# Token factor and shift applied to the result of two units at each norm boundary, and one unit per head pair moved from attention to the delta rule

## The chip, the cores and the metric

The kernel runs on one core of one Trainium2 chip. The metric is the device time of one execution in microseconds (us). Engines are named as in the profile: PE (TensorE; PEld its weight loads), DVE (VectorE), ACT (ScalarE), POOL (GpSimd), SP (SyncE, which issues the loads).

## The reference, cut to what matters

One decoder layer over 512 tokens of width 1024, all in float32:

```python
mod = cond @ w_ada[l] + b_ada[l]          # nine vectors: shift, scale, gate for each of three norms
u = modulate(rms_norm(h, g_ffn1[l]), sh1, sc1)            # rms_norm * (1 + scale) + shift
h = h + 0.5 * gt1 * swiglu(u, w_ffn1_in[l], w_ffn1_out[l])
u = modulate(rms_norm(h, g_mix[l]), sh2, sc2)
h = h + gt2 * hybrid_mixer(u, ...)        # stick-breaking attention | gated delta rule, merged by sigmoid gates
u = modulate(rms_norm(h, g_ffn2[l]), sh3, sc3)
h = h + 0.5 * gt3 * swiglu(u, w_ffn2_in[l], w_ffn2_out[l])
```

The mixer projects u to q, k, v of attention (8 heads of 64), to q, k, v, z, b, a of the delta rule (4 heads of 128) and to 2 x 1024 gate columns. For one token t, the modulated input is u = r(t) * (h * g * (1 + scale)) + shift, with one number r(t) per token. So a projection of it is u @ W = r(t) * ((h * g * (1 + scale)) @ W) + shift @ W.

## The kernel before, in words

Activations lie transposed: hT, u_hi and u_lo are [128 features, 8 chunks, 512 tokens]. Each matrix product is made of units. A unit is 128 output columns: its weights come by DMA into one of four `raw` slots, ACT rounds them to fp32r (`split_hi`, w_hi, L562), DVE forms the rest (`split_lo`, w_lo, L953), both into one of two slots, and PE runs three matmuls for each of 8 chunks (L1416 to L1418: w_hi u_hi, w_hi u_lo, w_lo u_hi; 11 chunks for a half unit of the FFN's second product). A unit's split waits until the unit two before it has freed the slot. Units have one numbering through the program: F1_IN, F1_OUT (first FFN), SB_IN (12 units: q, k, v of attention), DN_IN (the list MIXED: the delta rule's projections and the 16 gate units), MERGE, W_OUT, F2_IN, F2_OUT. Every engine has its own written-out program and meets the others at semaphores; SP issues the loads in the order of the units, each after the DVE split that frees its slot (`load_next`), and each gate unit's store before the load that follows it.

**Norm boundaries.** At F1_OUT to SB_IN and at W_OUT to F2_IN the next input needs the norm of the whole of h. After each output chunk DVE adds it to hT (`residual`, L1040) and ACT squares it (L569); POOL sums seven of eight squares. `statistics` makes two matmuls with 512 columns each (fp32, two passes each: L1427, L1429), which put the mean on all 128 partitions; `rough_root` (ACT, Ln and Exp, L574, L576) and `newton` (DVE, three operations, L990 to L994) work on [128, 512]. Then `norm` makes one chunk after another: `scaled` (DVE, L1027), u_hi (ACT, adds the shift, L593), `low` (DVE, u_lo, L1021), and `two_units` (L1445 to L1447) runs the first two units chunk by chunk as they come. While this goes on PE has nothing else.

**The conditioning vectors.** The 7168 late columns of w_ada are scaled by ACT (L582), halved by DVE (L961) and summed by PE (`ada_total`, L1434, one matmul for every four pieces); in F1_OUT that matmul stands between the two half units of every second output chunk.

**Attention.** For each of four head pairs: `scores` (L1614, L1618), then ACT's Abs, Exp, Ln and DVE's max-add (L1208), ACT's copy to att_hi (L766) and DVE's att_lo (L1214), then the log weights on PE (L1628), Exp (L770), the values (L1663), and ACT's and DVE's copy of y (L773, L1227). While PE waits for those it runs chunks of the MIXED units (`shadow`): 20 before the log weights, 6 before the values, 6 after them, four units for each pair. SHADOW holds these numbers; all three engines follow them through `pair_unit`.

**Delta rule.** Its stretch is serial work in small tiles: silu of the convolved q, k, v (ACT, L785, L786), l2 norms of q and k in four steps (squares L794, PE L1692, roots L807 and L811, DVE `newton` and L1244), transposes of v and k (L1700, L1708), then for each two blocks of 128 tokens the decay matrices, a triangular inverse in levels and the state steps. Between its steps PE runs the rest of MIXED: z units in the first three l2 steps, then gate units in numbers of chunks that the table FILL gives for each point; the class `filler` lets ACT and DVE make their part of a unit (split of the unit after next, eviction) when its eighth chunk is reached.

Of the kernel before, what the change touches and what calls it, by code (L numbers as in the profile page):

```python
# [54 lines left out]
    + [m for h in range(4) for m in (("conv", 5 + h), ("gate", h))] + [("z", h) for h in range(4)] \  # L55
    + [("gate", g) for g in range(4, 16)]
# [3 lines left out]
FILL_0 = Z_0 + 4  # L60
# [4 lines left out]
SHADOW = {"keep": 20, "weights": 6, "y": 6}  # L65
FILL = {"l2": 8, "start": 8, "prep": 7, "inv0": 2, "norm": 4, "level": 2, "join": 1, "solve": 2, "solved": 2, "step": 1, "last": 2}
# [22 lines left out]
def pair_unit(p, n):  # L89

    return PAIR_0 + 4 * p + n
# [34 lines left out]
def build(nc, x, c, w_ada, b_ada, g_ffn1, w_ffn1_in, w_ffn1_out, g_mix, w_in, g_q_sb, g_k_sb, w_conv,  # L126
# [13 lines left out]
    with ExitStack() as ctx:  # L140
# [28 lines left out]
        share = sb("share", [P, 1])  # L169
        ssq = sb("ssq", [P, S])  # L170
# [4 lines left out]
        with ExitStack() as s:  # L175
# [7 lines left out]
            tok = {n: sb("tok_" + n, [P, NB], stack=s) for n in ("sum", "mean", "rstd", "tmp")}  # L183
        with ExitStack() as s:
            g_hi, g_lo = sb("g_hi", [P, KF, S], f32r, stack=s), sb("g_lo", [P, KF, S], f32r, stack=s)
            with ExitStack() as t:
                ada_raw = sb("ada_raw", [P, 2, KD, P], stack=t)
            with ExitStack() as t:
                out_nat = sb("out_nat", [P, 2, NB, P], stack=t)
# [50 lines left out]

        def heads(ap):
# [45 lines left out]
        stat_ps, root_ready, rstd_ready, refined = sem("stat_ps"), sem("root_ready"), sem("rstd_ready"), sem("refined")  # L287
# [44 lines left out]
        def gate_buffer(g):  # L332

            return gate_out if g >= DNH and g % 2 else rstd
# [19 lines left out]
        def _(sp):  # L354
# [84 lines left out]
            for i in laps(sp, KD // 2, 0, 1):  # L439
                for u in range(4):  # L440
                    load_next(F1_OUT, i, u)
                    if not (is_static(i) and i == KD // 2 - 1 and u >= 2):
                        load_late(2 * KF + 4 * i + u - 2, u % 2)
            for n in range(SB_IN, F2_IN):
# [11 lines left out]
                if MERGE + 2 <= n < MERGE + KD:  # L456
                    sp.wait_ge(part_ready, 2 * (n - MERGE - 1))
                    stored(sp, n + 1 - MERGE + KD)
                    load_gates(n - MERGE)
            for phase, steps in ((F2_IN, KF // 2), (F2_OUT, KD // 2)):  # L460
# [6 lines left out]
        def _(pool):  # L467
# [38 lines left out]
            pool.wait_ge(u_lo_ready, 2 * KD)  # L506
# [41 lines left out]
        def _(act):  # L548
# [36 lines left out]
            def rough_root(s):  # L585
                act.wait_ge(stat_ps, s)
                inverse_root(rstd[:, :], 4, root_ready, s - 1)

            def norm_hi(s):
                rough_root(s)  # L590
                for k in range(KD):
                    act.wait_ge(normed_ready, KD * s + k + 1)
                    act.activation(u_hi[:, k, :], work[:, k % 2, :], ACT.Identity,  # L593
                                   bias=mod[:, SH[s] * KD + k:SH[s] * KD + k + 1]).then_inc(u_hi_ready, 1)

            def ffn(f, phase):

                for i in laps(act, KF // 2):
                    for jj in range(2):
# [72 lines left out]
            for i in laps(act, KD // 2):  # L672
                for oo in range(2):
                    split_hi(F1_OUT, i, 2 * oo + 2)
                    split_hi(F1_OUT, i, 2 * oo + 3)
                    squares(1, 2 * i + oo, oo)
                    if not (is_static(i) and i == KD // 2 - 1 and oo):
                        for k in range(2):
                            ada_scale(ada_raw[:, k], ada_scaled, (ada_in[k], 16 * (KF + 2 * i + oo)))
# [14 lines left out]

            for n in range(12):
                split_hi(SB_IN, 0, n + 2)
                act.wait_ge(unit_done, SB_IN + n + 1)
                act.activation(sb_T[:, n, :] if n < 8 else v_T[:, n - 8, :], bank(6 + n % 2), ACT.Copy).then_inc(proj_ready, 1)
# [13 lines left out]
            def mixed(m):  # L712
# [16 lines left out]
                else:  # L729
                    stored(act, d if d < DNH + 2 else d - 1)  # L730
# [19 lines left out]
            for p in range(SBH // 2):  # L750
# [20 lines left out]
                mixed(pair_unit(p, 2))  # L771
                act.wait_ge(y_ps, p + 1)
                act.activation(ysb_hi[:, p, :], region[0][:, 0:S], ACT.Copy).then_inc(y_hi_ready, 1)  # L773
                mixed(pair_unit(p, 3))
# [11 lines left out]
            act.activation(conv[:, 8:12, :], conv[:, 8:12, :], ACT.Silu).then_inc(dn_silu, 1)  # L786
            act.preload_act_table_set("natural_log_exp_and_others")
# [1117 lines left out]
```

## Time and profile before

| | us |
|---|---|
| median of 3 timed runs (lowest, highest) | 1314.07 (1313.59, 1314.76) |
| the profiled execution, its own time | 1316.56 |
| its span in the profile | 1314.8 |
| PE busy | 1261.0 (96%) |
| PE weight loads busy | 1012.2 (77%) |
| DVE busy | 646.7 (49%) |
| ACT busy | 604.9 (46%) |
| POOL busy | 61.9 (5%) |
| chain that ended last, PE's share | 87% |

The span is from the first to the last instruction of the profiled execution. Busy shares are of the span. The granted TensorE clock (PEclk) is a share of 2.4 GHz, and 0.5 of it is the lower level. Matmuls overlap, so their own durations are longer than the distance from one to the next. The page's slices show PE at 9 tenths or more nearly everywhere; the exceptions are the start, the two norm boundaries (near 420 and 940 us) and the delta rule (650 to 830 us).

### The profile page before, as it was taken

The page shows a single profiled execution, that of the slowest core. Times are in us where ns is not written, and L with a number is a line of the kernel's source. Part 1 is how long each engine was busy: PE and PEld are TensorE (multiplying, and loading weights), DVE is VectorE, ACT ScalarE, POOL GpSimd, SP SyncE. Part 2 cuts the span into 40 slices and gives each one's busy share as a digit, 9 for nine tenths or more (in the row PEclk, how much of TensorE's full clock was granted, in tenths as well). Part 3 has the DMA queues.
Part 4 walks back from the last instruction along what each step waited for, and adds up shares of the span by engine and source line. Part 5 has one row for each costly group of instructions (what it writes and reads, how often), then busy time and mean ns, then how long its engine had stood idle before and what let it go on. Part 6 is the DMA issues. An engine that isn't in the chain of part 4 may idle for free.

```text
span 1314.8 us, 18145 instructions
## 1 busy us (share of the span) xinstructions
PE 1261.0 (96%) x6637; PEld 1012.2 (77%) x6637; DVE 646.7 (49%) x927; ACT 604.9 (46%) x1101; POOL 61.9 (5%) x96
## 2 busy tenths in 40 slices
PE   6999999999997999999988999999799999999998
PEld 4778888887775777777767788787578888888887
DVE  4566666664445463665466366563533333332221
ACT  5476666664444455555664434553332222222211
POOL 0000000001110000000202021002000000000000
PEclk8999999999998999999989999999899999999999
DMA  9676777775652233222222110553133333333330
GB/s 312 188 199 183 191 191 191 188 206 149 163 150 56 64 80 81 65 64 81 81 57 65 50 49 26 160 176 96 49 96 96 96 96 98 98 116 109 104 89 25
DMA packets 278036, 152.38 MB, mean 116 GB/s; under 512 B 8005, under 2 KB 273374, under 8 KB 277982
## 3 DMA queue, kind: packets, MB, share of 16 engines
q1 hardware_dynamic: 273758, 149.54, 40.8%
q10 hardware_dynamic: 4224, 2.10, 0.5%
q8 instruction: 37, 0.61, 0.2%
q14 instruction: 17, 0.14, 0.0%
HBM read 145.31 MB, written 6.29 MB: 115 GB/s over the span
## 4 chain that ended last, share of the span: by engine, by line
PE 87%; ACT 5%; DVE 4%; issue 1%; DMA 1%; SPq 0%; ACTq 0%; DVEq 0%
PE tail L1416 12%; PE region L1416 12%; PE region L1417 12%; PE region L1418 12%; PE tail L1418 12%; PE tail L1417 12%; ACT ada_raw L582 2%; PE region L1628 2%; PE region L1434 1%; ACT w_hi L562 1%; PE region L1543 1%; PE region L1614 1%; PE region L1663 1%; PE region L1692 1%; DMA ada_early<-in_w_ada 1%
## 5 line engine op out<-in xcount | busy, mean ns | idle before, releaser
L562 ACT ACTIVATE w_hi<-raw 128x1024 fp32r<-128x1024 f32 (+1 forms) x177 | 197.7, 1117 | 519.6 <-PE tail L1418 275.8
L953 DVE TENSOR_TENSOR w_lo<-raw,w_hi 128x1024 fp32r<-128x1024 f32 (+1 forms) x177 | 229.5, 1297 | 276.2 <-ACT w_hi L562 274.6
L1416 PE MATMUL region<-u_hi,w_hi 128*128 128x512 f32 x656 | 259.2, 395 | 2.6 <-DVE w_lo L953 2.5
L1418 PE MATMUL region<-u_hi,w_lo 128*128 128x512 f32 x656 | 255.4, 389 | 0.0
L1417 PE MATMUL region<-u_lo,w_hi 128*128 128x512 f32 x656 | 255.4, 389 | 0.0
L1416 PEld LDWEIGHTS region<-u_hi,w_hi 128*128 128x128 f32 x656 | 123.1, 188 | 31.4 <-issue 5.0
L1416 PE MATMUL tail<-u_hi,w_hi 128*128 128x512 f32 x344 | 144.4, 420 | 1.9 <-DVE w_lo L953 1.9
L1417 PEld LDWEIGHTS region<-u_lo,w_hi 128*128 128x128 f32 x656 | 123.1, 188 | 27.6 <-issue 2.2
L1418 PEld LDWEIGHTS region<-u_hi,w_lo 128*128 128x128 f32 x656 | 123.1, 188 | 25.5
L1416 PE MATMUL tail<-g_hi,w_hi 128*128 128x512 f32 x352 | 141.7, 403 | 0.0
L1418 PE MATMUL tail<-g_hi,w_lo 128*128 128x512 f32 x352 | 139.2, 395 | 0.0
L1417 PE MATMUL tail<-g_lo,w_hi 128*128 128x512 f32 x352 | 139.2, 395 | 0.0
L1418 PE MATMUL tail<-u_hi,w_lo 128*128 128x512 f32 x344 | 135.5, 394 | 0.0
L1417 PE MATMUL tail<-u_lo,w_hi 128*128 128x512 f32 x344 | 135.5, 394 | 0.0
L582 ACT ACTIVATE ada_raw<-ada_raw,cond 128x128 f32<-128x128 f32 x448 | 134.1, 388 | 1.0 <-DMA ada_raw<-in_w_ada 1.0
L1059 DVE TENSOR_TENSOR work<-work,region 128x512 f32<-128x512 f32 x44 | 30.2, 687 | 112.1 <-PE region L1418 107.8
L961 DVE TENSOR_TENSOR ada_raw<-ada_raw 128x512 f32<-128x512 f32 x112 | 62.6, 559 | 41.8 <-ACT ada_raw L582 39.8
L1416 PEld LDWEIGHTS tail<-u_hi,w_hi 128*128 128x128 f32 x344 | 65.5, 190 | 19.7 <-issue 4.1
L1416 PEld LDWEIGHTS tail<-g_hi,w_hi 128*128 128x128 f32 x352 | 66.2, 188 | 16.7 <-issue 1.2
L1417 PEld LDWEIGHTS tail<-g_lo,w_hi 128*128 128x128 f32 x352 | 66.2, 188 | 16.6 <-issue 1.2
L1418 PEld LDWEIGHTS tail<-g_hi,w_lo 128*128 128x128 f32 x352 | 66.1, 188 | 16.0
L1417 PEld LDWEIGHTS tail<-u_lo,w_hi 128*128 128x128 f32 x344 | 65.3, 190 | 15.5 <-issue 3.4
(307 smaller groups left out, 1484.6 us busy)
## 6 DMA issues: line engine op xcount, KB each, us to landing
raw<-in_w_ffn_in SPq DMA_DIRECT2D x168, 256.0 KB, 3.3
ada_raw<-in_w_ada SPq DMA_DIRECT2D x56, 512.0 KB, 5.1
raw<-in_w_in SPq DMA_DIRECT2D x90, 256.0 KB, 3.3
raw<-in_w_ffn_out SPq DMA_DIRECT2D x32, 384.0 KB, 4.6
raw<-in_w_ffn_out SPq DMA_DIRECT2D x32, 320.0 KB, 4.0
ada_early<-in_w_ada SPq DMA_DIRECT2D x8, 1024.0 KB, 9.5
gates<-kept_gates SPq DMA_DIRECT2D x16, 256.0 KB, 4.2
raw<-in_w_out SPq DMA_DIRECT2D x16, 256.0 KB, 3.3
```

The lines of the kernel that those rows point to most:

```text
L562: act.activation(w_hi[:, slot % 2, 0:k, :], raw[:, slot, 0:k, :], ACT.Copy).then_inc(hi_ready, 1)
L582: ins = act.activation(piece[:, k, :], piece[:, k, :], ACT.Copy, scale=cond[:, k:k + 1])
L953: dve.tensor_tensor(w_lo[:, slot % 2, 0:k, :], raw[:, slot, 0:k, :], w_hi[:, slot % 2, 0:k, :].bitcast(f32), ALU.subtract).then_inc(lo_rea ...
L961: dve.tensor_tensor(dst, piece[:, 0:k, :], piece[:, k:2 * k, :], ALU.add).then_inc(done, 1)
L1059: dve.tensor_tensor(work[:, 1, :], work[:, 0, :], bank(2 * jj + 1), ALU.mult)\
L1416: pe.matmul(bank(b), wh, xh, start=start and n == 0, stop=False)
L1417: pe.matmul(bank(b), wh, xl, start=False, stop=False)
L1418: ins = pe.matmul(bank(b), wl, xh, start=False, stop=stop and n == k - 1)
L1434: pe.matmul(bank(5), ones[:, :], ada_acc.rearrange("p n e -> p (n e)"), start=True, stop=True)\
L1543: pe.matmul(dst, wh, xh, start=k == 0, stop=False)
L1614: pe.matmul(region[e][:, OFF[j]:OFF[j] + WID[j]], sb_T[rows_h, 2 * p + 1, j * P:(j + 1) * P], sb_T[rows_h, 2 * p, j * P:S], start=j < 3, s ...
L1628: ins = pe.matmul(region[e][:, at:at + WID[j2]], (neg_incl if j2 == j else neg_ones)[:, :], part[:, e, OFF[j2]:OFF[j2] + WID[j2]], start=F ...
```

## The change

*Norm boundaries.* While h is still being made, each chunk gets a plain input without token factor and shift: `plain_hi` and `plain_lo` write hT * scale_col into u_hi and u_lo. The first two units of the next phase run on these. Their result is multiplied by r(t) by DVE (`evict`, `late_pair`) and gets shift @ W as a bias. That bias is made by PE from the raw weights (`shift_parts`, 8 fp32 matmuls with 32 weight columns and 256 columns each, before or within the last unit of the phase before; `shift_totals`, 2 matmuls with one column). The statistics become 8 matmuls with one column, tokens on partitions; root and Newton steps work on [128, 4]; `spread_root` puts the root on all partitions by 4 matmuls. Unit 0 has the statistics inside (before chunk 3) and the root's spread before chunk 7; unit 1 follows chunk by chunk, and each chunk that it has used may be overwritten by the normed input. Units 2 and 3 run on the normed input in halves of four chunks (`late_units`). The table load for silu in the second FFN moves into `norm_hi(2)`, and the loop of W_OUT is written out. SP waits for `shift_parts` before it loads over the raw weights.

*F1_OUT.* `ada_total` moves behind the second half unit, except the last one.

*Attention and delta rule.* MIXED has the gate units last; pairs have three units (`pair_unit`), SHADOW 18, 3, 3. All of z1 to z3 and 16 gate units are fill. FILL: a new point `silu` with 12 chunks, `l2` now at three steps, `prep` 10 for 7, `solved` 5 for 2. The silu of v (128x2048) and the table load behind it move behind the first fill; the transposes of v go into the l2 steps 1 and 2, and those of k use four banks. Every odd gate unit is evicted to gate_out.

```diff
-    + [m for h in range(4) for m in (("conv", 5 + h), ("gate", h))] + [("z", h) for h in range(4)] \
-    + [("gate", g) for g in range(4, 16)]
+    + [("conv", 5 + h) for h in range(4)] + [("z", h) for h in range(4)] + [("gate", g) for g in range(16)]
-SHADOW = {"keep": 20, "weights": 6, "y": 6}
-FILL = {"l2": 8, "start": 8, "prep": 7, "inv0": 2, "norm": 4, "level": 2, "join": 1, "solve": 2, "solved": 2, "step": 1, "last": 2}
+SHADOW = {"keep": 18, "weights": 3, "y": 3}
+FILL = {"silu": 12, "l2": 8, "start": 8, "prep": 10, "inv0": 2, "norm": 4, "level": 2, "join": 1, "solve": 2, "solved": 5, "step": 1,
+        "last": 2}
...
 # ACT
+            def last_chunk(s, o):
+                copy_parts(s)
+                squares(s, o, 1)
+                plain_hi(s, o)
+                split_hi(late(s), 0, 1)
             def norm_hi(s):
-                rough_root(s)
+                act.wait_ge(stat_ps, s)
+                act.activation(tok["rstd"], bank(4)[:, 0:NB], ACT.Ln, bias=eps[:, 0:1]).then_inc(tok_root, 1)
+                act.activation(tok["rstd"], tok["rstd"], ACT.Exp, scale=-0.5).then_inc(tok_root, 1)
+                if s == 2:
+                    act.preload_act_table_set("silu_and_others")
+                split_hi(late(s), 0, 2)
                 for k in range(KD):
                     act.wait_ge(normed_ready, KD * s + k + 1)
+                    if k < KD - 1:
+                        act.wait_ge(plain_used, (KD - 1) * (s - 1) + k + 1)
+                    else:
+                        act.wait_ge(unit_done, late(s) + 2)
                     act.activation(u_hi[:, k, :], work[:, k % 2, :], ACT.Identity,
                                    bias=mod[:, SH[s] * KD + k:SH[s] * KD + k + 1]).then_inc(u_hi_ready, 1)
+                    if k == 3:
+                        split_hi(late(s), 0, 3)
...
 # DVE
+            def plain_lo(s, o):
+                dve.wait_ge(u_hi_ready, (2 * s - 1) * KD + o + 1)
+                dve.scalar_tensor_tensor(u_lo[:, ds(o, 1), :], hT[:, ds(o, 1), :], scale_col[:, s, ds(o, 1)],
+                                         u_hi[:, ds(o, 1), :].bitcast(f32), ALU.mult, ALU.subtract)\
+                    .then_inc(u_lo_ready, 1)
+            def evict(n):
+                dve.wait_ge(unit_done, SB_IN + n + 1)
+                dve.tensor_tensor(sb_T[:, n, :], bank(6 + n), rstd[:, :], ALU.mult).then_inc(late_ready, 1)
             def norm(s):
                 for k in range(KD):
                     if k >= 2:
                         low(s, k - 2)
-                    scaled(s, k)
+                    scaled(s, k, bank(4))
+                    if k == 1:
+                        split_lo(late(s), 0, 2)
+                        dve.tensor_copy(rstd[:, :], bank(4)).then_inc(rstd_ready, 1)
+                        if s == 1:
+                            evict(0)
+                    if k == 4:
+                        split_lo(late(s), 0, 3)
+                        if s == 1:
+                            evict(1)
...
 # PE
+            def late_units(s, banks):
+                def unit_0(k):
+                    if k == 3:
+                        statistics(s)
+                    if k == KD - 1:
+                        pe.wait_ge(u_lo_ready, plain + KD)
+                        spread_root(s)
+                unit(phase, 0, 0, banks[0], u_hi, u_lo, ready=unit_0).then_inc(unit_done, 1)
+                for k in range(KD):
+                    ins = unit(phase, 0, 1, banks[1], u_hi, u_lo, x0=k, w0=k, k=1, start=k == 0, stop=k == KD - 1)
+                    ins.then_inc(plain_used if k < KD - 1 else unit_done, 1)
+                for k0 in (0, 4):
+                    for u in (2, 3):
+                        ins = unit(phase, 0, u, banks[u], u_hi, u_lo, x0=k0, w0=k0, k=4, start=k0 == 0, stop=k0 == 4,
+                                   ready=lambda k: pe.wait_ge(u_lo_ready, normed + k0 + k + 1))
...
             for m in range(DNH):
-                if m < DNH - 1:
-                    mixed(Z_0 + 1 + m)
-                else:
-                    fill("l2")
+                fill("l2" if m else "silu")
                 for r in (2 * m, 2 * m + 1):
                     pe.wait_ge(l2_sq, r + 1)
...
+                if m in (1, 2):
+                    v_transposes(range(2 * m - 2, 2 * m))
             fill("start")
```

## Rows read from the trace of the kernel before

**Rows 1.** Waits of PE: line, who released it: us in total, times, longest

```profile
PE tail L1445 <- DVE u_lo L1021: 6.0, 1, 6.0
...
PE region L1692 <- ACT work L794: 5.5, 1, 5.5
...
PE region L1434 <- DVE ada_acc L961: 2.1, 4, 0.6
```

**Rows 2.** Stretches at boundary 1: length, busy us and count of each engine, PEclk, DMA

```profile
413.40:422.40 9.00, 2.16 (x5) 0.49 (x3) 6.34 (x10) 4.28 (x6) 0.00 (x0) 0.77 0.22 59
422.40:436.30 13.90, 13.84 (x48) 11.00 (x48) 9.48 (x16) 4.80 (x7) 0.10 (x1) 0.78 0.00 0
436.30:438.40 2.10, 0.15 (x2) 0.06 (x1) 1.23 (x1) 2.07 (x4) 0.00 (x0) 1.00 0.00 0
438.40:452.60 14.20, 14.20 (x53) 10.96 (x53) 5.28 (x6) 5.56 (x9) 0.00 (x0) 0.88 0.43 112
```

**Rows 3.** The same view at boundary 2.

```profile
931.80:940.80 9.00, 1.97 (x4) 0.31 (x3) 6.36 (x10) 4.39 (x6) 0.00 (x0) 0.79 0.25 72
940.80:953.30 12.50, 12.46 (x48) 9.99 (x48) 9.18 (x13) 4.79 (x7) 0.00 (x0) 0.88 0.00 0
953.30:955.30 2.00, 0.15 (x1) 0.01 (x1) 1.23 (x1) 1.97 (x3) 0.00 (x0) 1.00 0.00 0
955.30:966.20 10.90, 10.88 (x48) 9.02 (x49) 3.74 (x4) 3.55 (x5) 0.00 (x0) 1.00 0.40 118
```

**Rows 4.** The same view, one head pair and four stretches of the delta rule.

```profile
583.40:616.80 33.40, 33.40 (x179) 26.69 (x178) 16.54 (x17) 18.70 (x19) 0.00 (x0) 1.00 0.28 79
...
661.40:671.60 10.20, 10.18 (x28) 6.86 (x29) 6.15 (x9) 5.37 (x9) 0.00 (x0) 0.70 0.20 51
...
693.20:699.70 6.50, 4.23 (x33) 3.35 (x31) 3.05 (x4) 5.67 (x10) 0.00 (x0) 1.00 0.40 121
...
705.10:712.40 7.30, 5.07 (x24) 3.89 (x23) 7.07 (x20) 1.35 (x4) 3.71 (x4) 1.00 0.00 0
...
747.80:757.40 9.60, 7.49 (x43) 6.75 (x42) 3.50 (x7) 4.21 (x11) 0.00 (x0) 0.82 0.29 84
```

**Rows 5.** Groups by line and shape: busy us, mean ns of one, idle before.

```profile
L953 DVE TENSOR_TENSOR w_lo<-raw,w_hi 128x1024 fp32r<-128x1024 f32 x145 | 177.5, 1224 | 210.3 <-ACT w_hi L562 208.7
...
L562 ACT ACTIVATE w_hi<-raw 128x1024 fp32r<-128x1024 f32 x145 | 153.5, 1059 | 365.8 <-PE region L1418 224.3 <-PE tail L1418 131.7 <-PE tail L1447 4.7
...
L1021 DVE SCALAR_TENSOR_TENSOR u_lo<-work,mod,u_hi 128x512 fp32r<-128x512 f32 x24 | 17.9, 746 | 0.5
```

**Rows 6.** The chain that ended last, in order of time: start, us, line, count.

```profile
28.79 0.79 PE region L1530 x8
...
34.15 1.86 PE tail L1516 x32
...
445.70 0.86 PE region L1575 x2
...
600.56 5.53 PE region L1628 x40
...
760.18 0.89 PE region L1733 x8
```

**Rows 7.** ACT in order of time at the delta rule's start: start, us, line, tiles.

```profile
657.53 1.89 ACT L786 ACTIVATE conv<-conv 128x2048 f32<-128x2048 f32 x1
659.44 1.28 ACT L787 ACT_TABLE_LOAD   x1
660.74 1.15 ACT L794 ACTIVATE work<-conv 128x512 f32<-128x512 f32 x2
```

**Rows 8.** ACT and DVE in order of time in the same head pair.

```profile
596.76 2.67 ACT L766 ACTIVATE att_hi<-att_a 128x1280 fp32r<-128x1280 f32 x2 [0.40 <-DVE att_a L1208]
...
598.07 2.89 DVE L1214 TENSOR_TENSOR att_lo<-att_a,att_hi 128x1280 fp32r<-128x1280 f32 x2
...
606.12 1.24 ACT L770 ACTIVATE att_a<-region 128x1280 f32<-128x1280 f32 x1 [0.15 <-PE region L1628]
```

More of the change, by code:

```diff
@@ L913, in _ @@
             act.preload_act_table_set("natural_log_exp_and_others")
-            with act.Fori(0, 2) as i:
-                for u in range(4):
-                    split_hi(W_OUT, i, u + 2)
-                    squares(2, 4 * i + u, u % 2)
+            for o in range(KD):
+                split_hi(W_OUT, 0, o + 2) if o < KD - 1 else last_chunk(2, o)
+                if o < KD - 1:
+                    squares(2, o, o % 2)
+                    act.wait_ge(cols_ready, 4)
+                    plain_hi(2, o)
             norm_hi(2)
@@ L1235, in _ @@
             for m in range(DNH):
[L1236 to L1239 removed]
+                fill("l2" if m else "silu")
                 for r in (2 * m, 2 * m + 1):
@@ new lines, in statistics, with spread_root, shift_parts @@
+                ins.then_inc(stat_ps, 1)
+            def spread_root(s):
+                pe.wait_ge(tok_step, 4 + 3 * s)
+                for b in range(NB):
+                    ins = pe.matmul(bank(4)[:, b * P:(b + 1) * P], tok["rstd"][:, b:b + 1].to_broadcast([P, P]),
+                                    ident[:, :], start=True, stop=True)
+                ins.then_inc(tok_ps, 1)
+            def shift_parts(s):
+                slot = late(s) % RAW
+                for n in range(2):
+                    pe.wait_ge(raw_in[slot + n], raw_loads(late(s) + n))
+                pe.wait_ge(mod_ready, (SH[s] * KD + KD - LATE) // 4)
+                for k in range(KD):
+                    t = k % 4
+                    col = SH[s] * KD + k
+                    ins = pe.matmul(bank(3)[32 * t:32 * t + 32, 0:PIECE], mod[:, col:col + 1].to_broadcast([P, 32]),
+                                    raw[:, slot:slot + 2, k, :], start=k < 4, stop=k >= 4, tile_position=(0, 32 * t))
+                ins.then_inc(early_ps, 1)
@@ L1858, in _ @@
                          ready=(lambda k: pe.wait_ge(branch_lo, k + 1)) if o == 0 else None).then_inc(unit_done, 1)
-            with pe.Fori(0, 2) as i:
-                for u in range(4):
-                    pe.wait_ge(h_ready, 2 * KD + 4 * i + u - 1)
-                    unit(W_OUT, i, u, 6 + u % 2, m_hi, m_lo,
-                         ready=(lambda k: pe.wait_ge(branch_lo, DNH + k + 1)) if u == 0 else None)\
-                        .then_inc(unit_done, 1)
-            statistics(2)
+            for o in range(KD):
+                pe.wait_ge(h_ready, 2 * KD + o - 1)
+                if o == KD - 1:
+                    shift_parts(2)
+                unit(W_OUT, 0, o, 6 + o % 2, m_hi, m_lo,
+                     ready=(lambda k: pe.wait_ge(branch_lo, DNH + k + 1)) if o == 0 else None).then_inc(unit_done, 1)
+            shift_totals(2)
             ffn_in(1, F2_IN)
```

282 lines of the change are left out of this document (188 added, 94 removed).

## The prediction

> **What bounds the kernel now.** The page comes first: TensorE (PE) is busy 96% of the span and has 87% of the chain that ended last, VectorE (DVE) 49%, ScalarE (ACT) 46%, the DMA engines a quarter to three quarters. Only two things can shorten it: PE's idle time, and the time in which PE runs at its lower clock. The waits of PE come second; there the reader sees two equal waits of 6.0 us, one at each norm boundary (L1445; one row stands for both), 5.5 us at the first l2 statistics of the delta rule (L1692), and 2.1 us at L1434 [rows 1]. Third come stretches with the granted clock; they show two more idle times in the delta rule, 2.2 us in 705.1 to 712.4 and 2.1 us in 747.8 to 757.4. Most idle times are followed by a clock below 1.00: 0.78 over 13.9 us, 0.88 over 14.2, 0.70 over 10.2, 0.82 over 9.6 (its idle time included), 0.88 over 12.5 [rows 2 to 4]. The levels are 1.2 and 2.4 GHz, so (1 minus PEclk) times length is what PE lost there: 3.1 + 1.7 + 3.1 + 1.7 + 1.5 = 11.1 us.
>
> At full clock 48 matmuls take 10.9 us [rows 3]: 0.227 us each, 0.68 us for a chunk (three matmuls), 5.45 us for a unit of eight chunks. All sums below use this pace; the sum of the change is made against the profiled execution (1316.56 us, span 1314.8).
>
> **Boundary 1 (first FFN to mixer).** Before, the last matmul of the FFN ends at 413.4 and unit 4 of the mixer starts at 452.6: 39.2 us for four units (21.8 us at pace) [rows 2]. What PE executes after the change between these points: four units 21.8; `shift_totals`, four passes; `statistics`, sixteen passes with one column each; `spread_root`, eight passes like L1733; two head statistics. Passes like the first two took 0.79 us for eight, `spread_root`'s form 0.89, a head statistic 0.86 [rows 6]: 0.4 + 1.6 + 0.9 + 1.7. Sum 26.4 us.
>
> Waits, counted from the last matmul T. A weight split is 1.06 us on ACT and 1.22 on DVE, a u chunk 0.75 on DVE [rows 5] and a little less on ACT, an eviction on DVE I take as 0.7. Unit 0 runs on chunks 0 to 2 from T+0.4, the statistics end at T+4.1 (the last square is out by T+1.7), root and three corrections now have 4 columns and are done by T+5.6, `spread_root` ends at T+8.0, unit 0 at T+8.6, unit 1 at T+14.1. DVE's queue is what PE meets next: scaled 0 and 1 (T+9.7), split of unit 2 (waits for unit 0 to free its slot, T+11.1), root copy, evict 0, low 0 (T+13.2), then a chunk each 1.45 us: low 1 T+14.7, low 2 T+16.2. Behind scaled 4 stand the split of unit 3 and evict 1 (T+19.3), so low 3 comes at T+20.0. PE, in units 2 and 3 by halves, wants low 2 at T+15.5 and low 3 at T+17.0: it waits 0.75 + 3.1 us; from then on it has 13 chunks (8.9 us) against 5.0 us of DVE work, so it waits no more. Unit 4's split on DVE ends about T+30, near the two head statistics' end: no further wait.
>
> After a 2.1 us idle time at 436.3 the clock fell (0.88 over the 14.2 us behind it, 1.7 us lost) [rows 2]; after 2.0 us at 953.3 it stayed 1.00 [rows 3]. For the 3.1 us wait I charge 1.7, for one near 2.4 us half of it. Boundary 1: 26.4 + 3.9 + 1.7 = 32.0, plus `shift_parts` (sixteen passes, 1.86 for 32 [rows 6], 0.9) in the FFN's last unit: gain 39.2 - 32.9 = **6.3 us**.
>
> **Boundary 2 (mixer to second FFN).** Before: 931.8 to 966.2, 34.4 us [rows 3]. After: 21.8 + 0.4 + 1.6 + 0.9 = 24.7; the same queue without evictions makes low 3 late by 2.5 us (low 2 is in time); clock 0.9; unit 4's split comes 0.2 late, since ACT does the silu first; `shift_parts` 0.9. Gain 34.4 - 29.2 = **5.2 us**. W_OUT unrolled and `plain_hi`/`plain_lo` (0.75 us a chunk on ACT and DVE) hide beside units of 5.45 us; without that cover 0.75 a chunk.
>
> **F1_OUT.** Three of four `ada_total` move behind the second half unit. Their waits (2.1 us for four [rows 1]) go: +1.6. The fourth stays, and `plain_hi`, `plain_lo` now stand ahead of what it waits for: -0.7. **+0.9 us**.
>
> **Attention.** 32 chunks (21.8 us) leave, and come back as fill: nothing by itself, if PE is still the bound. A pair is 33.4 us, PE busy in all of it [rows 4]; with 8 chunks fewer it is 27.9. PE reached the log weights (5.53 us, in four parts) of pair 2 at 600.56 [rows 6], after 20 chunks; two chunks less bring it there at 599.2 and to the second part at 600.6, where the first copy is done about 598.1, the second at 599.4 and both low parts at 600.96 [rows 8], before the third. The values wait for a second Exp (1.24 [rows 8]) that starts when the log weights end, beside three chunks of 2.04: 0.7 us in hand. The next scores wait for ACT's copy of y and DVE's low part (0.6 and 0.7, less than a u chunk each), beside the same three chunks: 0.6 in hand. So 0. Below nothing it can't go, PE has no idle time there.
>
> **Delta rule.** `fill("silu")` gives PE 12 chunks (8.2 us) where it had 8 (5.45), and the big silu (1.89) with its table load (1.28) goes behind the squares [rows 7]. Before, the squares came 5.5 us late; they now come 5.5 - 2.7 - 3.2 = -0.4, in time: wait and low clock (3.1) go, 8.6 us. What is late next: the big silu and the load now stand ahead of the Ln of the first l2 pair, so the next squares come about 1.0 us after PE's 8 chunks. The v transposes leave the end, where they covered DVE's last l2 corrections: that stretch was 6.5 us with 4.2 busy [rows 4]; now k's transposes wait about 2.4 us for DVE, then 0.8 for ACT's copies: equal, -0.1, and half a clock fall, -0.8. Sum **6.7 us**. `prep` gets 3 chunks more for each pair of blocks (2.0 us) against an idle time of 2.2 [rows 4] and about half of it at the second pair of blocks, but its splits now push ACT's copies and DVE's products by 1.5 and 0.6: **+1.0**. `solved` gets 3 more against 2.1 us idle and 1.7 us of low clock (0.82 over 9.6 [rows 4]); v_new comes 0.7 later behind a split, a wait of 1.0 is left: **+2.8**. The 38 chunks left at the end run at pace; gates 0 to 3 now use the alternating buffer, their stores (256 KB) have a unit's time each.
>
> *A rule that speaks against this.* Between the table load at 659.44 (1.28 us) and the square at 660.74 lie 0.02 us [rows 7]. The Trainium skill (ScalarE: Activation LUTs, What ACT_TABLE_LOAD costs) gives a switch of sets a drain of 1.38 us on top of the load; by that the second squares would be 1.4 us later and the gain 1.4 us less, while the load that `norm_hi(2)` now does would still be hidden. This trace shows no such drain, so the sum has none.
>
> **Sum.** 6.3 + 5.2 + 0.9 + 6.7 + 1.0 + 2.8 = 22.9 us. 1316.56 - 22.9 = 1293.7 for a profiled execution; the timed runs lie 2.5 lower (median 1314.07): **1291 us**. Bounds of what isn't seen: a one-column pass between 0.06 us (L1516's) and 0.43 (half a head statistic) [rows 6], so the statistics 0.9 to 6.9 us at each boundary; 0.1 is taken because L1530's has the same shape, and the far end is left to the rivals; clock falls between none (-3.4 against the sum) and all, each as long as the longest seen (3.1 us; +6); the DVE chunk between 0.7 and 0.8. Own range 1284 to 1299.
>
> **Rivals.**
>
> A, deeper gain: no clock fall, `spread_root` and queue a little quicker. For it: 2.0 us of idle time without a fall at 953.3. Against: the clock fell after five others. 22.9 + 3.4 + 2: about 1286 us. 13%.
>
> B, the delta rule is held by ACT and DVE: their serial chain, now with more splits and evictions within it, keeps PE idle as before and only the silu wait goes; each boundary loses the long clock fall of before again (3.1 in place of 1.7 or 0.9). For it: DVE is busy 7.1 of the 7.3 us ahead of L1754 [rows 4]. Against: in the other stretches of these rows it is busy half of the time. The gains of `solved` (2.8) and `prep` (1.0) go, the clock falls in the l2 part after all (3.1), the boundaries lose 3.6, extra splits cost 2: 22.9 - 12.5 leaves 10.4, about 1304 us. 20%.
>
> C, slower: attention becomes ACT- and DVE-bound. Place: the keep chain (Abs, Exp, Ln, max-add, copy, low part) before the log weights. If it, not PE, sets the pair's pace, each pair stays near 33.4 us while its 5.45 us of chunks run elsewhere: 21.8 us given back, and each of four idle times brings a clock fall of 1.7: 1291 + 21.8 + 6.8 = 1320 us. It decides from a shortfall of 23 / 4 = 5.7 us a pair, where I see 0.6 in hand. Against: busy sums, ACT 18.7 and DVE 16.5 of 33.4 us [rows 4]. 5%.
>
> D, the plain chunks don't run ahead: if unit 0 had to wait for the root after all, both boundaries keep their waits (12 us) and the new passes come on top. For it: nothing but that u_hi is written twice. 1291 + 11.5 + twice the new passes (3.8) less the old statistics (1.7): about 1307 us. 4%.
>
> **How the numbers follow.** Forecast 58%, A 13, B 20, C 5, D 4. From 1282 to 1304 lie the forecast's own range, nearly all of A and half of B, whose upper half, C and D are left out: about 0.8. What a measurement of this kernel can tell from no change is about 0.2% (2.6 us). Faster 0.94, same 0.02, slower 0.04.
>
> **What would show it.** The waits at L1445 gone, and one of 2 to 4 us inside the second pair of units, on DVE's u_lo of chunk 3, at both boundaries; statistics of 1.6 us; the pairs of attention at 27.9 us without PE idle; L1692 without its first wait, a small one at the second pair, one of about 2.4 us before k's transposes; clock loss near 3.4 us in all where it was 11.1. Wrong if a pair takes over 28.5 us, if the boundaries keep more than 5 us of idle time each, or if the time is above 1304.

## The result and the profile after

| | before | after |
|---|---|---|
| median (lowest, highest), four runs each | 1314.41 (1313.59, 1316.76) us | 1285.34 (1285.04, 1285.43) us |
| the profiled execution, its own time | 1316.56 | 1285.04 |
| its span | 1314.8 | 1283.1 |
| mean granted clock of the span | 0.986 | 0.997 |

The ratio of the times is 0.9776, 95% interval 0.9759 to 0.9793: faster by 29 us. The forecast was 1291.0, its range 1282 to 1304. Direction and range held; the profiled executions lie 31.5 us apart where the sum had 22.9.

The waits of PE after, in the columns of [rows 1]. The 6.0 us at the boundaries, the 5.5 at the first l2 statistics and three of the four short ones of `ada_total` are gone. In their place:

```profile
PE tail L1564 <- DVE u_lo L1135: 3.1, 2, 2.6
...
PE region L1975 <- ACT dn_prod L919: 2.7, 3, 0.9
PE region L1564 <- DVE u_lo L1135: 2.0, 1, 2.0
PE region L1903 <- DVE conv L1388: 1.6, 1, 1.6
...
PE region L1636 <- DVE ada_acc L1037: 1.3, 1, 1.3
...
PE region L1928 <- ACT k_dn L893: 0.9, 1, 0.9
PE region L2032 <- DVE ssq L1490: 0.8, 1, 0.8
...
PE region L1894 <- ACT work L869: 0.2, 1, 0.2
```

The first row is boundary 1, the third boundary 2. L1903 is k's transposes, L1928 the decay matrices behind them, L2032 the point `solved`, L1894 the second l2 statistics (the first have no wait), L1975 a step of the triangular inverse, L1636 the last `ada_total` of F1_OUT.

Stretches after, in the columns of [rows 2]: four of boundary 1, one of boundary 2, a head pair, and the whole delta rule.

```profile
410.30:424.90 14.60, 14.60 (x80) 12.52 (x79) 9.14 (x15) 5.44 (x9) 0.00 (x0) 1.00 0.28 73
424.90:427.50 2.60, 2.12 (x8) 0.97 (x6) 2.29 (x4) 1.88 (x4) 0.00 (x0) 1.00 0.00 1
427.50:430.10 2.60, 0.00 (x1) 0.00 (x0) 2.50 (x4) 0.64 (x2) 0.00 (x0) 1.00 0.07 11
430.10:442.00 11.90, 11.90 (x44) 9.17 (x44) 6.49 (x11) 6.58 (x10) 0.10 (x1) 0.86 0.17 43
...
909.30:926.90 17.60, 16.41 (x86) 13.57 (x85) 11.87 (x18) 9.24 (x13) 0.00 (x0) 1.00 0.21 61
...
562.10:590.00 27.90, 27.90 (x153) 22.12 (x152) 17.96 (x20) 17.16 (x17) 0.00 (x0) 1.00 0.21 57
...
617.90:817.90 200.00, 191.72 (x1836) 157.77 (x1835) 112.79 (x213) 97.53 (x190) 31.47 (x58) 1.00 0.24 71
```

And the delta rule of before, from the end of attention to the merge:

```profile
650.10:840.30 190.20, 174.66 (x1740) 143.01 (x1739) 108.71 (x209) 91.84 (x182) 30.34 (x52) 0.97 0.20 57
```

Boundary 1 is 31.7 us in place of 39.2 [rows 2]: PE is busy in all of it but 0.5 and 2.6 us, then it loses 0.14 x 11.9 = 1.7 us to the lower clock. The pair is 27.9 us in place of 33.4 [rows 4], PE busy throughout. The delta rule got 32 chunks (21.8 us) more and became only 9.8 us longer: PE's idle time fell from 15.5 to 8.3 us, and the low clock (0.03 x 190, over 5 us) went. At boundary 2 the clock stayed at 1.00.

DVE's queue around the long wait, in order of time (start, us, line, tiles). PE stands from 427.5 to 430.1:

```profile
425.74 0.75 DVE L1135 SCALAR_TENSOR_TENSOR u_lo<-work,mod,u_hi 128x512 fp32r<-128x512 f32 x1
426.52 0.75 DVE L1141 SCALAR_TENSOR_TENSOR work<-hT,scale_col,region 128x512 f32<-128x512 f32 x1
427.56 1.23 DVE L1029 TENSOR_TENSOR w_lo<-raw,w_hi 128x1024 fp32r<-128x1024 f32 x1 [0.29 <-ACT w_hi L580]
428.70 0.68 DVE L1102 TENSOR_TENSOR sb_T<-tail,rstd 128x512 f32<-128x512 f32 x1
429.30 0.74 DVE L1135 SCALAR_TENSOR_TENSOR u_lo<-work,mod,u_hi 128x512 fp32r<-128x512 f32 x1
```

Low 2, scaled 4, split of unit 3, evict 1, low 3: the order of the prediction (0.29 us of it is the split waiting for ACT's w_hi). Low 3 ended 19.7 us behind the last matmul of F1_OUT; 20.0 were forecast.

### The profile page after: what moved, and what is told of

Its sections match the earlier page's. It is cut to its first block, busy times and chain, and to the rows that moved or that the text cites. A ratio compares the mean times of both kernels' runs of the same rounds, so it can differ in the third digit from the quotient of the medians.

```text
span 1283.1 us, 18316 instructions
## 1 busy us (share of the span) xinstructions
PE 1250.5 (97%) x6717; PEld 1012.4 (79%) x6717; DVE 670.0 (52%) x951; ACT 612.1 (48%) x1119; POOL 62.8 (5%) x96
## 4 chain that ended last, share of the span: by engine, by line
PE 89%; DVE 5%; ACT 4%; issue 1%; DMA 1%; SPq 1%; ACTq 0%; DVEq 0%
PE tail L1564 13%; PE region L1564 13%; PE region L1566 13%; PE region L1565 12%; PE tail L1566 12%; PE tail L1565 12%; PE region L1820 2%; PE region L1636 1%; ACT w_hi L580 1%; DVE w_lo L1029 1%; PE region L1735 1%; PE region L1806 1%; PE region L1855 1%; ACT ada_raw L600 1%; PE region L1975 1%
## 5 line engine op out<-in xcount | busy, mean ns | idle before, releaser
L1564 PE MATMUL region<-u_hi,w_hi 128*128 128x512 f32 x672 | 265.8, 396 | 2.7 <-DVE u_lo L1135 2.0
L1566 PE MATMUL region<-u_hi,w_lo 128*128 128x512 f32 x672 | 261.7, 389 | 0.0
L1565 PE MATMUL region<-u_lo,w_hi 128*128 128x512 f32 x672 | 261.6, 389 | 0.0
L1564 PE MATMUL tail<-u_hi,w_hi 128*128 128x512 f32 x360 | 149.5, 415 | 3.3 <-DVE u_lo L1135 3.1
L1564 PEld LDWEIGHTS region<-u_hi,w_hi 128*128 128x128 f32 x672 | 126.1, 188 | 32.1 <-issue 2.7
L1565 PEld LDWEIGHTS region<-u_lo,w_hi 128*128 128x128 f32 x672 | 126.2, 188 | 28.1 <-issue 2.2
L1566 PEld LDWEIGHTS region<-u_hi,w_lo 128*128 128x128 f32 x672 | 126.1, 188 | 26.5
L1566 PE MATMUL tail<-u_hi,w_lo 128*128 128x512 f32 x360 | 141.3, 392 | 0.0
L1565 PE MATMUL tail<-u_lo,w_hi 128*128 128x512 f32 x360 | 141.1, 392 | 0.0
L1566 PEld LDWEIGHTS tail<-u_hi,w_lo 128*128 128x128 f32 x360 | 67.9, 189 | 14.9
L1037 DVE TENSOR_TENSOR ada_raw<-ada_raw 128x512 f32<-128x512 f32 x112 | 62.5, 558 | 31.8 <-ACT ada_raw L600 29.4
L1565 PEld LDWEIGHTS tail<-g_lo,w_hi 128*128 128x128 f32 x352 | 66.1, 188 | 15.5 <-issue 1.0
```

Of the source, the lines that this page charges most:

```text
L1037: dve.tensor_tensor(dst, piece[:, 0:k, :], piece[:, k:2 * k, :], ALU.add).then_inc(done, 1)
L1564: pe.matmul(bank(b), wh, xh, start=start and n == 0, stop=False)
L1565: pe.matmul(bank(b), wh, xl, start=False, stop=False)
L1566: ins = pe.matmul(bank(b), wl, xh, start=False, stop=stop and n == k - 1)
```

## The experiments

Times are medians; before was 1314.8 to 1315.8 us in the same sets, and each ratio is to it. The length of a stage is the distance between the first matmuls of two stages in the trace of the one profiled execution of each kernel. Edits are cut to the lines that matter; "..." and comments mark what is left out.

**The boundary part alone**, and **the attention and delta-rule part alone**. The first keeps MIXED, SHADOW, FILL, `pair_unit`, gate buffers and the order of the l2 steps of before; the second has only these edits.

```diff
-SHADOW = {"keep": 18, "weights": 3, "y": 3}      # boundary part alone: back to 20, 6, 6; FILL and MIXED too
-            late_units(1, (6, 7, 6, 7))          # delta part alone: back to statistics(1), two_units
...
```

> The kernel before with the norm-boundary part of the change and the edits of F1_OUT alone; MIXED, SHADOW, FILL and the delta rule's order stay as they were. Theory 1 (the parts add up, and a moved buffer address adds its own gain): by the prediction's terms 6.3 + 5.2 + 0.9 = 12.4 us, and about 5.5 us more because the new small tiles in front of g_hi move its address (a matmul's pace in F1_OUT, W_OUT and F2_OUT falls from 0.233 to 0.228-0.230 us): 1314.4 - 17.9, about 1296.5 us. Rival 1 (no address effect; the 6 us that the change gained over the forecast come from the delta rule or from clock falls between the parts): 1302 us. Rival 2 (boundaries gain less than their terms and the delta rule made the rest): above 1304 us. In the trace: a wait of 2 to 3 us for chunk 3's low part at each boundary, the delta rule's idle times as before (5.5 us at the first l2 statistics).

> The kernel before with the attention and delta-rule part of the change alone; boundaries, F1_OUT and W_OUT as before, all buffer addresses as before. Theory 1: the prediction's terms 6.7 + 1.0 + 2.8 = 10.5 us, and about 1.5 more since two of the waits charged (1.0 and 0.8 us) came out smaller: 1302 to 1304 us, matmul pace in F2_OUT still 0.233 us. Rival 1 (the surplus of 6 us is in this part): 1298 us. Rival 2 (the part gains only the silu wait and its clock fall): 1306 us or more.

Measured: 1298.63 us, ratio 0.9869 (0.9849 to 0.9889), and 1303.16 us, ratio 0.9915 (0.9902 to 0.9929): 17.2 and 12.7 us less than before, together 29.9. The whole change gave 29.1. Within their intervals (some 2.5 and 2 us) the parts add up. The traces say it more sharply: the first kernel's stages gained 2.7 us in F1_OUT, 7.3 at boundary 1 and 2.2 in F2_OUT, each as in the whole change, and 5.7 in boundary 2 and F2_IN, where the whole change had 7.3 and no clock fall; attention and delta rule of the second gained 11.5 where the whole change had 12.1. With 12.7 us for the second kernel two of its rivals fall: that the surplus over the forecast lies in it (1298 us), and that it gains only the silu wait (1306 us or more). The first kernel's 1298.6 lies between its theory (1296.5, with an address effect) and its rival (1302, without) and can't tell them apart; the next experiment does. The second kernel's waits of PE in the delta rule are those of the whole change within 0.2 us:

```profile
PE region L1779 <- ACT dn_prod L846: 2.7, 3, 0.9
PE region L1707 <- DVE conv L1240: 1.8, 1, 1.8
PE region L1732 <- ACT k_dn L820: 0.9, 1, 0.9
PE region L1836 <- DVE ssq L1342: 0.8, 1, 0.8
```

**An unused tile in front of ssq.** In before, F1_OUT's matmuls start 0.2333 us apart, after 0.2289; F2_OUT, whose code is the same, is 2.2 us shorter. The change puts small tiles (`tok`, `late_bias`) ahead of the large ones and so moves g_hi by 96 bytes, with `ssq`, `work`, g_lo, m_hi and m_lo. The experiment moves them alone.

```diff
+        sb("gap", [P, 24])      # before + 96 bytes; after + 64 (16) and + 192 (48)
         ssq = sb("ssq", [P, S])
```

> The kernel before with one unused tile of 96 bytes per partition in front of ssq, which puts ssq, work, g_hi, g_lo, m_hi and m_lo at the addresses that they have in the changed kernel (g_hi from 127840 to 127936); no instruction changes. Theory 1 (the pace of a matmul depends on where its moving operand lies): F1_OUT 528 matmuls and F2_OUT 528 by 0.005 us each, W_OUT and the merge some 0.5 together: about 1309 us, pace 0.228 us in F1_OUT and F2_OUT. Rival (the pace follows from the loop's form, the traffic beside it or the position of the instructions): 1314.4 us, pace 0.233.

> The changed kernel with one unused tile of 64 bytes per partition in front of ssq: g_hi, g_lo, m_hi and m_lo start at multiples of 128 bytes, as u_hi and u_lo do (g_hi 128000 for 127936). Theory 1 (address): the pace in F1_OUT, W_OUT and F2_OUT falls to the 0.2268 us of the loops that read u_hi and u_lo, 0.0015 us on 1250 matmuls: 1283.3 us, 2 us less than the changed kernel. Rival (no address effect, or one that 64 bytes have already exhausted): 1285.3 us.

> The changed kernel with one unused tile of 192 bytes per partition in front of ssq: g_hi 128128, so that g_hi minus w_hi (88192) is a multiple of 512 bytes, as u_hi minus w_hi (32896) is. So far the pace of a matmul was 0.2333 us at a difference of 224 bytes modulo 512 (before), 0.2283 at 320 (after), 0.2325 at 384 (the 64-byte tile), 0.2268 at 0 (all loops on u_hi and u_lo). Theory 1 (the difference modulo 512 between moving operand and weights decides, 0 is best): pace 0.2268 in F1_OUT and F2_OUT, time 1283.5 us, 2 us under the changed kernel. Theory 2 (the address alone decides, not the difference; 320's value was luck): a pace between 0.228 and 0.233 and 1285 to 1292 us. Rival (the tile itself makes it slower, as the 64-byte tile seemed to): 1292 us.

Measured: 1309.68 us (ratio 0.9962, 0.9948 to 0.9975), 1292.10 us (0.9823, 0.9810 to 0.9837) and 1285.16 us (0.9771, 0.9758 to 0.9785). The same stage, F2_OUT, in five kernels (length, then PE's busy time and count; PE never waits in it): before,

```profile
1184.00:1309.60 125.60, 125.60 (x553) 101.42 (x552) 31.01 (x25) 24.14 (x22) 0.00 (x0) 1.00 0.28 81
```

before with 96 bytes more,

```profile
1180.00:1303.50 123.50, 123.50 (x553) 101.44 (x552) 31.01 (x25) 24.14 (x22) 0.00 (x0) 1.00 0.29 82
```

after,

```profile
1154.40:1277.90 123.50, 123.50 (x553) 101.42 (x552) 31.01 (x25) 24.14 (x22) 0.00 (x0) 1.00 0.28 82
```

after with 64 bytes more,

```profile
1159.40:1285.10 125.70, 125.70 (x553) 101.38 (x552) 31.00 (x25) 24.16 (x22) 0.00 (x0) 1.00 0.28 81
```

after with 192 bytes more:

```profile
1154.60:1277.10 122.50, 122.50 (x553) 101.40 (x552) 31.02 (x25) 24.14 (x22) 0.00 (x0) 1.00 0.29 83
```

Of the 6.1 us that 96 bytes gave, 5.0 lie in F1_OUT, merge, W_OUT and F2_OUT; of the 6.8 that 64 bytes cost, 4.8 lie there and 1.6 in a clock fall at boundary 2. No instruction differs between the first two, or among the last three; only addresses do. g_hi minus w_hi modulo 512 is 224, 320, 320, 384 and 0 bytes; the pace in the middle of F1_OUT is 0.2333, 0.229, 0.229, 0.2327 and 0.2270 us, the last that of every loop on u_hi, whose difference is 0 too. The tiles of ACT and DVE move too, but their traffic isn't the cause: between those matmuls of F2_OUT beside which ACT, DVE and POOL all stood still (297 distances) the mean pace was 0.2333, 0.2288, 0.2288, 0.2333 and 0.2267 us. So the address effect is shown, and my guess that a multiple of 128 bytes is what matters is refuted. Whether the difference to the weights or g_hi's own residue modulo 512 (352, 448, 448, 0 and 128; u_hi's is 128) decides is open: in the best kernel both are those of u_hi. Its median gained nothing: 2.2 us came in F1_OUT, merge, W_OUT and F2_OUT, but in the profiled run the low clock at boundary 1 lasted 6.8 us (428.3 to 435.2) where after had 3.4. At like clock the gain is there: its run at mean clock 0.997 took 1282.88 us, the changed kernel's 1285.04; three others at 0.995 took 1285.16 to 1285.75.

**DVE's order at the boundaries.** Units 2 and 3 of boundary 1 go to banks 2 and 3, and PE no longer waits for the evictions ahead of them, so that these can come last. The split of unit 3 moves behind low 3 at both boundaries.

```diff
-                        if s == 1: evict(0)           # at k == 1
-                    if k == 4: split_lo(late(s), 0, 3), evict(1)
+                        if k == 5: split_lo(late(s), 0, 3)      # behind low(s, 3)
+                if s == 1: evict(0), evict(1)                   # behind the last low
-                        if s == 1 and k0 == 0: pe.wait_ge(late_ready, u)
-            late_units(1, (6, 7, 6, 7))
+            late_units(1, (6, 7, 2, 3))
```

> The changed kernel with DVE's queue at both boundaries in another order: units 2 and 3 of the first boundary use banks 2 and 3, both evictions stand behind the last low part, and the split of unit 3 stands behind low 3 in place of ahead of it. Theory 1 (the prediction's: chunk 3's low part is late because split and eviction stand ahead of it): at the first boundary the waits of 0.3 and 2.6 us give way to 0.6 at unit 3's split and about 0.6 at chunks 6 and 7, and the half clock behind them (1.7 us) goes: 3.3 us; at the second 2.0 us of waiting gives way to 1.1: 0.9 us. Together 1281.1 us. Rival (ACT's u_hi or the spread of the root sets the pace, not DVE's queue): the wait stays within 0.5 us and the time is 1285 us.

Measured: 1282.12 us, ratio 0.9750 (0.9737 to 0.9763). Boundary 1 in this kernel, from F1_OUT's end at 411.6 to unit 4 at 440.4, takes 28.8 us (31.7 after), and the clock stays up:

```profile
411.60:429.00 17.40, 16.91 (x88) 14.04 (x88) 11.97 (x19) 7.96 (x12) 0.00 (x0) 1.00 0.23 61
429.00:430.00 1.00, 0.83 (x4) 0.35 (x4) 1.00 (x2) 0.00 (x0) 0.00 (x0) 1.00 0.00 0
430.00:440.40 10.40, 10.13 (x40) 6.95 (x38) 7.19 (x13) 7.05 (x11) 0.11 (x1) 1.00 0.19 50
```

It waits 1.0 us in all at boundary 1 and 0.7 at boundary 2. Theory 1 holds: DVE's queue, not the root or ACT, made chunk 3 late. The stage from F1_OUT's end to the first scores is 3.2 us shorter. At boundary 2, where the waits fell from 2.0 to 0.7 us and no clock fall was there to lose, the stage is only 0.6 us shorter. Part of the wait is left in pieces too short for that list: between 922 and 935 us seven matmuls of PE start 0.30 to 0.34 us ahead of the next where 0.227 is usual, against two at the same place of the changed kernel.

**Thinner cover in attention.**

```diff
-SHADOW = {"keep": 18, "weights": 3, "y": 3}
+SHADOW = {"keep": 22, "weights": 1, "y": 1}
```

> The changed kernel with SHADOW 22, 1, 1 for 18, 3, 3: one chunk (0.68 us) beside the second Exp and one beside y in place of three (2.04 us). Theory 1 (the prediction's margins of 0.7 us at the values and 0.6 us at the next scores): 1.36 us fewer chunks leave a wait of 0.7 us at the values and 0.8 at y, 1.5 us for each of four pairs, 6 us in all: 1291 us, and up to 3 more where the clock falls. Rival 1 (the margins are much larger, attention is far from ACT and DVE): 1285 to 1287 us. Rival 2 (there is no margin left, ACT and DVE set the pair's pace already): 2.7 us a pair, 1296 us or more.

Measured: 1291.89 us, ratio 0.9828 (0.9813 to 0.9843). Waits of PE from the first scores to the end of attention, where the changed kernel has none:

```profile
PE region L1855 <- ACT att_a L843: 2.3, 4, 0.6
PE region L1806 <- DVE ysb_lo L1375: 1.6, 3, 0.5
PE region L1873 <- DVE ysb_lo L1375: 0.5, 1, 0.5
```

With 1.36 us less cover the values wait 0.6 (2.3 in four) and y 0.5 (2.1 in four): margins of 0.8 us both, where the prediction had 0.7 and 0.6. Attention took 4.9 us more, where 6 were expected; the rest is a clock fall at boundary 2 (PE at the lower clock from 932.6 to 936.0).

**Eight chunks at `silu`**, and **the big silu first**.

```diff
-FILL = {"silu": 12, ...
+FILL = {"silu": 8, ...
```

```diff
+            act.activation(conv[:, 8:12, :], conv[:, 8:12, :], ACT.Silu).then_inc(dn_silu, 1)
+            act.preload_act_table_set("natural_log_exp_and_others")
             for m in range(DNH):                 # the same two lines leave the step m == 0
```

> The changed kernel with 8 chunks of fill ahead of the first l2 statistics in place of 12, the four chunks run later. Theory 1 (the prediction's sum: the squares would be 2.3 us late with 8 chunks, and 12 cover them by 0.4): a wait of about 2.3 us at the first l2 statistics, and some of a clock fall: 1287.6 to 1289 us. Rival (most of the gain at this point came from moving the big silu, four more chunks bring nothing): 1285.3 us.

> The changed kernel with the silu of v and the table load ahead of the first squares again, as before the change; 12 chunks of fill stay. Theory 1 (the prediction's: it puts 3.2 us of ACT ahead of the squares, whose margin is 0.4 us with 12 chunks): a wait of 2.8 us at the first l2 statistics, the 0.2 us at the second squares go; together about 2.6 us and up to 1.7 for a clock fall: 1288 to 1290 us. Rival (the margin is larger, the twelve chunks alone had hidden the wait): at most 1286 us.

Measured: 1286.75 us (ratio 0.9787, 0.9772 to 0.9802) and 1290.49 us (0.9811, 0.9798 to 0.9825). Both theories' waits came as computed: 2.3 us with 8 chunks,

```profile
PE region L1894 <- ACT work L869: 2.7, 2, 2.3
PE region L1903 <- DVE conv L1388: 2.1, 1, 2.1
...
PE region L1975 <- ACT dn_prod L919: 0.9, 1, 0.9
```

and 2.8 with the silu first, with a clock fall behind it (PE at the lower clock from 629.4 to 632.8):

```profile
PE region L1893 <- ACT work L871: 2.8, 1, 2.8
PE region L1974 <- ACT dn_prod L918: 2.7, 3, 0.9
```

Yet 8 chunks cost only 1.4 us, less than the 2.3 to 3.7 expected and no more than the two intervals leave open, and in the profiled run the way from the end of attention to the merge was as long as after (200.0 us). The four chunks ran later and found idle time there: the waits for dn_prod fell from 2.7 to 0.9 and the one for ssq went. With the silu first that way was 3.7 us longer, 2.6 of it waiting.

**Twelve chunks at `start`.** If a late chunk is free, cover ahead of k's transposes should be had for nothing.

```diff
-FILL = {..., "start": 8, ...
+FILL = {..., "start": 12, ...
```

> The changed kernel with 12 chunks of fill in place of 8 at the point start, ahead of k's transposes; the unit boundaries of all later fill move by four chunks, to where they are with 8 chunks at silu. Theory 1 (fill is a stock that is worth something only where PE would be idle, and ACT's and DVE's share of a unit costs where it falls into the serial chain): the wait of 1.6 us ahead of k's transposes goes, and as with 8 chunks at silu the waits for dn_prod (2.7 us in three) fall to 0.9 and that for ssq (0.8) goes: 4.2 us, 1281 us. Rival 1 (only the cover counts): 1.6 us, 1283.7 us. Rival 2 (the chunks are missed later by as much): 1285.3 us.

Measured: 1282.13 us, ratio 0.9754 (0.9741 to 0.9768). Waits of PE in the delta rule:

```profile
PE region L1928 <- ACT k_dn L893: 1.9, 1, 1.9
PE region L1975 <- ACT dn_prod L919: 0.9, 1, 0.9
```

The rows for L1903 and L2032 are gone; L1928 kept 1.0 us more of it than expected, so 3.2 us came of 4.2; the delta rule in the trace is 3.4 us shorter (196.6 for 200.0). Rivals 1 (1.6 us) and 2 (nothing) fall: where a unit of fill ends in the serial chain, and with it the split and the eviction that stand ahead of ACT's next copy, counts as much as how many chunks cover a point.

**`ada_total` back between the half units**, on PE alone.

```diff
+                        if f == 0 and oo == 1:
+                            ada_total(KF // 2 + i - 1)      # last or not
                         if last:
-                            ada_total(KF // 2 + i - 1)
...                                                          # behind the second half unit
-                        if f == 0 and oo == 1:
-                            shift_totals(1) if last else ada_total(KF // 2 + i - 1)
+                        if last:
+                            shift_totals(1)
```

> The changed kernel with the three moved ada_total matmuls back between the two half units, on PE alone. Theory 1 (the prediction's term): the waits for ada_acc come back, 2.1 to 2.7 us for four in the kernels before, of which 1.3 is there already, and plain_hi and plain_lo push what they wait for by 0.7 us for each: 0.8 + 3 x 0.7, about 3 us in F1_OUT: 1288 us. Rival (ACT and DVE have room in F1_OUT, the place of the matmul is worth nothing): 1285.3 us.

Measured: 1290.73 us, ratio 0.9815 (0.9801 to 0.9828). The waits in F1_OUT went from 1.3 to

```profile
PE region L1636 <- DVE ada_acc L1037: 5.1, 4, 1.3
```

and F1_OUT took 4.6 us more from its first to its last matmul, where about 3 were expected. Each of the four waits is 1.3 us: the three come on top of the one that was there, 3.8 us and not 3. The median rose by 5.4 us; the profiled run has a clock fall of 1.6 at boundary 2 besides.

**Three edits together**: DVE's order, 192 bytes, 12 chunks at `start`.

> The changed kernel with three edits of this study together: DVE's order at the boundaries as in evicts_late, g_hi at the same residue as w_hi and u_hi (192 bytes further), 12 chunks at start. Theory 1 (the gains add up): 3.2 measured for the first, 2 us of matmul pace for the second (0.0015 us on some 1250 matmuls, without a clock fall at the first boundary to blur it), 1.6 to 4.2 for the third: 1276 to 1278.5 us. Rival (clock falls elsewhere take the gain back): 1280 us or more.

Measured: 1277.35 us (1275.24 to 1278.18), ratio 0.9711 (0.9697 to 0.9724): 8.0 us under the changed kernel, 37 under before. The three medians by themselves gained 3.2, 0.2 and 3.2 us, 6.6 in all. In the trace the stages are shorter by 3.1 and 0.5 us at the boundaries, 2.2 in F1_OUT, merge, W_OUT and F2_OUT, and 2.4 in the delta rule. So DVE's order and the address keep their gains, and that of the address shows in the time now, as expected, with no clock fall at boundary 1. The 12 chunks gave 1.1 less than alone: behind the same wait of 1.9 us for k_dn the clock fell here (661.4 to 664.8) and not there.

## Why the prediction was right, and what it missed

The sum was right in most of its terms; one that it lacked, the address, made most of the surplus. Stage by stage in the two traces, gains in us. The split of the last column into address and the rest uses the kernel with 96 bytes more:

| stage | forecast | measured | of it address |
|---|---|---|---|
| F1_IN | 0 | 0.4 | |
| F1_OUT (edits +0.9, `shift_parts` -0.9) | 0 | 2.7 | 1.7 |
| boundary 1 to the first scores | 7.2 | 7.3 | |
| attention, less 32 chunks | 0 | 0.1 | |
| delta rule, plus 32 chunks | 10.5 | 12.0 | |
| merge and W_OUT (`shift_parts` -0.9) | -0.9 | -0.1 | 1.1 |
| boundary 2 and F2_IN | 6.1 | 7.3 | |
| F2_OUT | 0 | 2.2 | 2.2 |
| sum | 22.9 | 31.8 | 5.0 |

*Boundary 1* was right in mechanism and size. The statistics took 1.7 us (1.6 forecast: the one-column pass is 0.1 us, not 0.43), the wait sat on chunk 3's low part (2.6 for 3.1, and 0.5 on chunk 2 for 0.75), and it brought the clock fall of 1.7 us. That it came in this run was likely, not certain: one of nine such kernels had none. Moving DVE's queue moved it.

*Boundary 2* was mis-sized by 1.2: the wait was 2.0, not 2.5, and no clock fall followed, where half of one (0.9) was charged. The charge was fair: of nine kernels profiled with this wait of 2.0 us, five show a fall behind it and four none.

*Attention* was right. The margins were computed at 0.7 and 0.6 and are 0.8 both.

*Delta rule.* The first squares are exact: 2.3 and 2.8 us of waiting where the prediction's margin of 0.4 gave these numbers. Charged too high were the second squares (1.0; it is 0.2), k's transposes (2.4; 1.6) and the clock (0.8; no fall). `prep` came out at its +1.0: its own waits for DVE fell from 3.4 to 0.2 us, and the 2.1 charged for splits ahead of ACT's copies and DVE's products came back as 2.1 at dn_prod, which is late three times (0.6 us before, 2.7 after). That place wasn't named, nor that it depends on where units of fill end; `start_twelve` takes 1.8 of it away. `solved` gained 1.3 of waiting and 1.7 of clock, 3.0 for 2.8.

*F1_OUT.* The 0.7 us charged for `plain_hi` and `plain_lo` ahead of the last total are right: its wait went from about 0.5 to 1.3. The edits still brought 1.0 more than the terms. In the kernel with 96 bytes more the four old waits are 2.7 us, not 2.1, so three of them are 2.0 and not 1.6; the rest, 0.6, isn't traced to a row. That plain chunks and totals must not both stay ahead of the second half unit is shown: it would have cost 4.6 us.

*The step that was not in the sum* is the largest: I took PE's pace as one number, 0.227 us, from a loop on u_hi, and a moved buffer as nothing. 5.0 of the 8.9 us missed are this. The trace of before had the sign of it, in F1_OUT's 0.2333.

*The offset.* I carried 2.5 us from the profiled run of before to the median. That was no property of profiled runs: before took 1315.7 to 1316.7 us in the twelve later runs at mean clock 0.986 and 1313.0 to 1314.8 in the ten at 0.988, and its profiled run was of the first kind; the changed kernel's profiled run is within 0.3 us of its median. Without the offset the forecast would have been 1293.7. That a wrong term brought the number nearer was luck: the gain was 31.5 us in the profiled runs for a sum of 22.9, and the forecast of 1291 missed by only 5.7.

*Rivals.* A had the size nearest (1286), but its reason, no clock fall, holds at boundary 2 and in the delta rule and not at boundary 1; the kernel with DVE's order changed is what A described. B fell on the delta rule's waits, C on the pairs, D on unit 0, which started at 410.7, nearly seven us ahead of the root's spread (417.4).

*The rule weighed.* ACT after, in order of time:

```profile
627.76 1.91 ACT L876 ACTIVATE conv<-conv 128x2048 f32<-128x2048 f32 x1
629.69 1.28 ACT L877 ACT_TABLE_LOAD   x1
630.98 1.27 ACT L882 ACTIVATE dn_link<-region,eps 128x512 f32<-128x512 f32 x2
```

The load stands 0.02 us behind the silu and 0.01 ahead of the Ln: again no drain beside it. The 1.38 us that the Trainium skill (ScalarE: Activation LUTs, What ACT_TABLE_LOAD costs) adds are not in this trace, and the second squares, 0.2 us late, leave no room for them.

## What to carry to other kernels

When statistics hold up a product, let the first units run on the input without them and correct the result; then read the queue of the engine that corrects, for what stands ahead of the next chunk is the new wait. Fill is a stock: place it by where PE idles and by where its side work falls in the serial chain, not by cover alone. Before pricing anything, measure the matmul pace of each loop: where two loops of the same shape differ, try the address. Compare stages of the traces as well as medians: here they repeated within 0.1 us from kernel to kernel where nothing had changed and the clock was the same, while the medians carried the clock falls of other stages.

## What the runs showed of the hardware

The same 512-column fp32r matmuls started 0.2270, 0.229, 0.2327 or 0.2333 us apart when an unused tile moved their moving operand in SBUF: 2.5% of F2_OUT (122.5 against 125.7 us), and 7.1 us over F1_OUT, merge, W_OUT and F2_OUT between 192 and 64 bytes of it.

The lower clock comes and goes in one and the same program. The boundary part alone took 1295.42, 1295.46, 1298.63, 1298.84 and 1301.25 us at mean clocks of 0.993, 0.993, 0.990, 0.990 and 0.989. In the nine profiled kernels that have the changed boundaries and DVE's first order, the wait of 2.6 us at boundary 1 was followed by a fall in eight and that of 2.0 us at boundary 2 in five; where DVE's order was changed (waits of 0.2 to 0.5 us, two kernels) by none at either. A fall lasted 3.4 us at half the clock there, once 6.8, and the short one cost 1.6 to 1.7: from F1_OUT's end to the first scores the changed kernel took 96.1 us, and 94.6 in the one kernel of the nine without a fall. So removing a wait gives back, in some runs, that much besides. In the delta rule a wait of 1.9 us was followed by a fall in one kernel (`combined`) and not in another (`start_twelve`).
